# The last layer normalisation of a two-block network: its scaling step divided anew between three engines

## The chip, the cores and the metric

The kernel runs on one core of a Trainium2 chip. The metric is the device time of one execution in microseconds, lower is better. The version before takes 1869.55 us (median of three runs, 1868.58 to 1870.9 us).

## The reference

The program runs two networks one after the other on 512 tokens of width 1024, all in float32: a state-space layer and an attention layer with their feed-forward parts, then two layers of mixed attention. The second network ends each layer with a layer normalisation, and the last of them gives the output. Cut to what matters here:

```
def _layernorm(t, g, b):
    mu = jnp.mean(tf, -1, keepdims=True)
    var = jnp.mean(jnp.square(tf - mu), -1, keepdims=True)
    out = (tf - mu) * lax.rsqrt(var + LN_EPS) * g + b
...
for layer in range(DEPTH):
    ...
    y = jnp.einsum('bse,ed->bsd', jnp.concatenate([ya, yb, yc], axis=-1), w_out[layer])
    h = _layernorm(DEEPNORM_ALPHA * h + y, ln_g[layer], ln_b[layer])
return h
```

## The kernel before

Activations are kept transposed: the 1024 features lie on 128 partitions in eight tiles, `xT[:, k, :]` for k from 0 to 7, each 128 partitions by 512 tokens. So the gain `g` and the shift `b` of a tile are one number for each partition (`column(name, k)`, a column of `vecs`), while mean and root differ along the 512 tokens. The mean over features is a product with a matrix of ones on TensorE, which leaves the same row on all partitions: bank 7 gets the sum that corrects the mean, bank 6 the sum of squares.

Each engine has its own written-out order of instructions, and they meet at semaphores. The normalisation `layer_norm(m, ...)` is called three times, m = 0, 1, 2. Only the last call (`last`) is changed, and it is the end of the program. Its work after the last product of the output projection is this.

- ScalarE copies the correction of the mean from bank 7 to `acc` (L1044), squares it (L1046), and later makes the root in `R` from the variance in `sd`: a logarithm (L701) and an exponential (L702), both in `inverse_root`.
- "Levelling" subtracts the correction of the mean from a tile. VectorE does it from bank 7 for tiles 0, 1, 2, 3 and 7 (`level`, L1813), GpSimd from `acc` for tiles 4, 5 and 6 (L613, `POOL_LEVELS`). VectorE makes the variance between its second and third levelling (L1834).
- VectorE then scales all eight tiles in order: `xT = xT * gain * R` in one instruction each (`scale`, L1821), with the levelling of tile 7 after the scaling of tile 3.
- ScalarE adds the shift to each tile as it has been scaled (L1053).
- SyncE sends each tile to the output as its shift has been added (L509): eight transfers of 256 KB, in order 0 to 7. It then waits for all of them, which ends the program.

In the calls that are not last, the loop over tiles also makes two halves of each tile for the next product; the change leaves these as they are.

Of the kernel before, what the change touches and what calls it, by code (L numbers as in the profile page):

```python
# [18 lines left out]
ACT = mybir.ActivationFunctionType  # L19
ALU = mybir.AluOpType  # L20
# [5 lines left out]
KD = D // P  # L26
# [118 lines left out]
def build(nc, x_in, pos, vec, con, ssm_par, ssm_b, ssm_c, ssm_d, w_in, w_glu, w_gu0, w_dn0, w_a, w_q, w_k, w_v, w_o, w_gu1, w_dn1,  # L145
# [21 lines left out]
    n = 0  # L167
# [13 lines left out]
    xT = everywhere.tensor("xT", [P, KD, S])  # L181
# [4 lines left out]
    tiny = everywhere.tensor("tiny", [P, 64])  # L186
# [4 lines left out]
    R = common.tensor("R", [P, S])  # L191
    VM = Region(nc, common.base + common.at, 8 * KB).tensor("VM", [P, 2, QP, P])
    acc = common.tensor("acc", [P, S])
    sd = common.tensor("sd", [P, S])
# [28 lines left out]
    def column(name, k=0):  # L223
        return vecs[:, VEC[name] + k:VEC[name] + k + 1]
# [92 lines left out]
    sp = Region(nc, common.base, 10 * KB).tensor("sp", [P, 2, 10 * P])  # L317
# [34 lines left out]
    wbfL = common.tensor("wbfL", [P, 2, KD * 4], F32R)  # L352
    CENTRED = (0, 1, 3, 2, 4, 5, 6, 7)
    POOL_LEVELS = (4, 5, 6)
    square_sum = T[:, 0, :]
    squares = (sq[:, 0, :], sq[:, 1, :], T[:, 1, :], T[:, 2, :])
    lat = Oall[:, :, :].rearrange("p a b -> p (a b)")
# [35 lines left out]
    with ExitStack() as ctx:  # L393
        sems = {}

        def sem(name):
            if name not in sems:
                sems[name] = ctx.enter_context(nc.semaphore(name))
            return sems[name]

        banks = [ctx.enter_context(nc.psum_tensor(f"bank{n}", [P, S], F32)) for n in range(8)]
# [9 lines left out]
        def _(sp):  # L411
# [92 lines left out]
                for name in ("qk", "v", "mixed", "out"):  # L504
                    stream(f"{name}{layer}")

            for j in range(KD):
                sp.wait_ge(sem("ln_h"), 8 * 2 + j + 1)
                sp.dma_start(out[j * P:(j + 1) * P, :], xT[:, j, :]).then_inc(sem("out_written"), 16)  # L509
            sp.wait_ge(sem("out_written"), 16 * KD)  # L510

# [1 line left out]
        def _(pool):  # L513
            step = Steps(pool, sem("pool_steps"))
# [94 lines left out]
            def level(m):  # L609
                pool.wait_ge(sem("ln_delta_copied"), m + 1)  # L610
                pool.wait_ge(sem("ln_sq"), 8 * m + 8)
                for k in POOL_LEVELS:
                    nc.gpsimd.tensor_tensor(xT[:, k, :], xT[:, k, :], acc[:, :], ALU.subtract).then_inc(sem("ln_levelled"), 1)  # L613

            for layer in range(2):
# [25 lines left out]
                def add_later(side, to, a, b):  # L641
                    return nc.gpsimd.tensor_tensor(later[:, side, to:to + P], sp[:, side, a:a + P], b, ALU.add)

                pool.wait_ge(sem("shares_ready"), 2 * STEPS * (layer + 1))
                for p in range(2):
# [5 lines left out]
                    for side in range(2):  # L651
# [2 lines left out]
                        add_later(side, P, SOFF[1] + P, sp[:, side, SOFF[2]:SOFF[2] + P])  # L654
                        add_later(side, 2 * P, SOFF[1] + 2 * P, later[:, side, 0:P]).then_inc(sem("stick_later"), 1)
            level(2)

        @block.scalar
        def _(act):
            def ahead(st, i, u, last):  # L660

                v = u + 2
                if v >= st.n:
                    v -= st.n
                    if not last:
                        i = i + 1
                    elif st.name in following:
                        st, i = following[st.name], 0
                    else:
                        return  # L670
                split_high(st, i, v)
# [8 lines left out]
            step = Steps(act, sem("act_steps"))  # L680
# [18 lines left out]
            def inverse_root(o, bank, scale, made, eps=0):  # L699

                step(nc.scalar.activation(o, bank, ACT.Ln, scale=scale, bias=tiny[0:o.shape[0], eps:eps + 1]))  # L701
                nc.scalar.activation(o, o, ACT.Exp, scale=-0.5).then_inc(made, 1)  # L702
# [319 lines left out]
            def layer_norm(m, name, last=False):  # L1022
                st = stages[name]
                blocks = 3 if name.startswith("dn") else 1
                nc.scalar.preload_act_table_set("natural_log_exp_and_others")

                def centred_square(n):
                    at = CENTRED.index(n)
                    act.wait_ge(sem("ln_centred"), 8 * m + at + 1)
                    if at >= 4:  # L1030
                        act.wait_ge(sem("ln_sq_used"), 7 * m + at - 3)
                    nc.scalar.activation(squares[at % 4], xT[:, n, :], ACT.Square).then_inc(sem("ln_sq"), 1)

                for n in range(KD):
                    for b in range(blocks):
                        if n < KD - 1 or b < blocks - 1:
                            ahead(st, n // 4, n % 4 * blocks + b, n >= 4)
                    if n == 2:
                        act.wait_ge(sem("ln_part"), m + 1)
                        nc.scalar.activation(sd[:, :], banks[7][:, :], ACT.Copy, scale=1.0 / (2 * P)).then_inc(sem("ln_mean"), 1)  # L1040
                    for k in {3: (0, 1, 3), 4: (2, 4), 5: (5,), 6: (6,), 7: (7,)}.get(n, ()):
                        centred_square(k)
                act.wait_ge(sem("ln_delta"), m + 1)
                nc.scalar.activation(acc[:, :], banks[7][:, :], ACT.Copy, scale=1.0 / D).then_inc(sem("ln_delta_copied"), 1)  # L1044
                act.wait_ge(sem("ln_delta_copied"), m + 1)
                nc.scalar.activation(sd[:, :], acc[:, :], ACT.Square).then_inc(sem("ln_delta_square"), 1)  # L1046
                act.wait_ge(sem("ln_variance"), m + 1)
                inverse_root(R[:, :], sd[:, :], 1.0, sem("ln_root"), eps=1)
                shift = ("ln_in_b", "ln_b0", "ln_b1")[m]
                for k in range(KD):  # L1050
                    act.wait_ge(sem("ln_scaled"), 8 * m + k + 1)
                    if last:
                        nc.scalar.activation(xT[:, k, :], xT[:, k, :], ACT.Identity, bias=column(shift, k)).then_inc(sem("ln_h"), 1)  # L1053
                        continue
                    nc.scalar.activation(xH[:, k, :], xT[:, k, :], ACT.Identity, bias=column(shift, k)).then_inc(sem("ln_high"), 1)
                    if k == 4:
                        ahead(st, 1, 4 * blocks - 1, True)

            def evict(st, i, u, to, func=ACT.Copy):
                ahead(st, i, u, i == st.turns - 1)  # L1060
                act.wait_ge(w_used, st.block(i, u) + 3)
                return nc.scalar.activation(to, banks[(tiles[st.name] + u) % 4][:, :], func)

            layer_norm(0, "dn1")
            for layer in range(2):
                st = stages[f"qk{layer}"]
# [87 lines left out]
                for s in range(STEPS):  # L1154
                    m, j = divmod(s, QT)
# [65 lines left out]
                stick_weights(1, 2)  # L1221
                gated_high(7)
                layer_norm(layer + 1, f"out{layer}", layer == 1)

        @block.vector
        def _(dve):
            step = Steps(dve, sem("dve_steps"))
# [314 lines left out]
            for i in range(st.turns):  # L1542
                for u in range(st.n):
                    ahead(st, i, u, i == st.turns - 1)
                    if u % 3 == 2:
                        j = 4 * i + u // 3
# [95 lines left out]
            scale = 1.0 / math.sqrt(DN + DR)  # L1642
# [106 lines left out]
            def layer_norm(m, name, bank_of, last=False):  # L1749
                gain, shift = (("ln_in_g", "ln_g0", "ln_g1")[m], ("ln_in_b", "ln_b0", "ln_b1")[m])  # L1750
# [61 lines left out]
                def level(k):  # L1812
                    nc.vector.scalar_tensor_tensor(xT[:, k, :], banks[7][:, :], -1.0 / D, xT[:, k, :], ALU.mult, ALU.add)\  # L1813
                      .then_inc(sem("ln_level"), 1)

                def scale(k):
                    if k in POOL_LEVELS:
                        dve.wait_ge(sem("ln_levelled"), 3 * m + POOL_LEVELS.index(k) + 1)
                    else:
                        dve.wait_ge(sem("ln_level"), 5 * m + min(k, 4) + 1)  # L1820
                    nc.vector.scalar_tensor_tensor(xT[:, k, :], xT[:, k, :], column(gain, k), R[:, :], ALU.mult, ALU.mult)\  # L1821
                      .then_inc(sem("ln_scaled"), 1)

                def low(k):
                    dve.wait_ge(sem("ln_high"), 8 * m + k + 1)
                    nc.vector.scalar_tensor_tensor(xL[:, k, :], xT[:, k, :], column(shift, k), xH[:, k, :].bitcast(F32),
                                                   ALU.add, ALU.subtract).then_inc(h_ready, 1)
# [7 lines left out]
                level(2)  # L1835
                level(3)
                dve.wait_ge(sem("ln_root"), m + 1)
                for k in range(KD):
                    scale(k)
                    if k and not last:  # L1840
                        low(k - 1)
                    if k == 3:
                        level(KD - 1)
                if last:
                    return
                low(KD - 1)
                block_ahead(KD - 1, blocks - 1)
                dve.wait_ge(h_ready, 56 + 16 * m)
# [2 lines left out]
                dve.wait_ge(sem("ln_h"), 8 * m + 8)  # L1851

            layer_norm(0, "dn1", lambda n: banks[(tiles["dn1"] + n) % 4][:, :])
            for layer in range(2):
                lam, sub_gain = tiny[:, 20 + layer:21 + layer], tiny[:, 22 + layer:23 + layer]
# [37 lines left out]
                bias = vecs[0:4, VEC[f"bf{layer}"]:VEC[f"bf{layer}"] + 1]  # L1893
# [63 lines left out]
                for s in range(STEPS):  # L1957
                    m, j = divmod(s, QT)
# [868 lines left out]
```

## Time and profile before

| what | value |
|---|---|
| median of three runs | 1869.55 us (1868.58 to 1870.9) |
| the profiled execution's own time | 1869.21 us |
| its span, first to last instruction | 1867.2 us |
| outside the span | 2.0 us |
| TensorE busy | 1821.6 us, 98% of the span |
| VectorE, ScalarE, GpSimd busy | 1046.7, 838.0, 199.7 us |
| first scaling of the last normalisation starts | 1857.68 us |
| first and last output transfer issued | 1859.45 and 1864.7 us |

The span is the profiled execution's time from its first instruction to its last; the two differ by what lies around it. Busy times are sums of the durations of an engine's instructions, which can overlap by some hundredths of a microsecond when one follows the other without a wait. A number such as L1821 is a line of the kernel before.

### The profile page before, as it was taken

The page shows a single profiled execution, that of the slowest core. Times are in us where ns is not written, and L with a number is a line of the kernel's source. Part 1 is how long each engine was busy: PE and PEld are TensorE (multiplying, and loading weights), DVE is VectorE, ACT ScalarE, POOL GpSimd, SP SyncE. Part 2 cuts the span into 40 slices and gives each one's busy share as a digit, 9 for nine tenths or more (in the row PEclk, how much of TensorE's full clock was granted, in tenths as well). Part 3 has the DMA queues.
Part 4 walks back from the last instruction along what each step waited for, and adds up shares of the span by engine and source line. Part 5 has one row for each costly group of instructions (what it writes and reads, how often), then busy time and mean ns, then how long its engine had stood idle before and what let it go on. Part 6 is the DMA issues. An engine that isn't in the chain of part 4 may idle for free.

```text
span 1867.2 us, 24330 instructions
## 1 busy us (share of the span) xinstructions
PE 1821.6 (98%) x8918; PEld 1407.2 (75%) x8918; DVE 1046.7 (56%) x1633; ACT 838.0 (45%) x1402; POOL 199.7 (11%) x269
## 2 busy tenths in 40 slices
PE   9999999999999999999999999989999989999997
PEld 6787878888887766677888888768666767866675
DVE  8893454444334767755444434465565476556647
ACT  5323344443224667644434422232467633255753
POOL 7880000000000000000000000023000112200000
PEclk9989999999999999999999999999999999999998
DMA  6222223232333111122232333323111122311111
GB/s 211 77 84 79 91 90 101 90 101 91 94 100 103 44 34 28 61 68 93 98 98 93 100 93 94 97 87 99 64 50 53 46 90 88 104 50 54 57 45 57
DMA packets 58764, 152.21 MB, mean 82 GB/s; under 512 B 17152, under 2 KB 22048, under 8 KB 58672
## 3 DMA queue, kind: packets, MB, share of 16 engines
q1 hardware_dynamic: 55120, 148.27, 24.9%
q0 software_dynamic: 3552, 2.70, 0.5%
q8 instruction: 59, 0.97, 0.2%
q14 instruction: 33, 0.27, 0.0%
HBM read 143.79 MB, written 4.19 MB: 79 GB/s over the span
## 4 chain that ended last, share of the span: by engine, by line
PE 91%; DVE 5%; ACT 3%; issue 1%; DMA 0%; POOL 0%; DVEq 0%; SPq 0%; ACTq 0%
PE bank L2018 19%; PE bank L2019 19%; PE bank L2020 19%; PE bank L2511 3%; PE bank L2513 3%; PE bank L2512 3%; PE bank L2488 2%; PE bank L2476 2%; PE bank L2475 2%; PE bank L2474 2%; PE bank L2243 1%; PE bank L2271 1%; PE bank L2598 1%; PE bank L2526 1%; DVE wl L1244 1%
## 5 line engine op out<-in xcount | busy, mean ns | idle before, releaser
L1244 DVE TENSOR_TENSOR wl<-raw,wh 128x1024 fp32r<-128x1024 f32 (+3 forms) x280 | 327.0, 1168 | 492.9 <-ACT wh L677 489.7
L677 ACT ACTIVATE wh<-raw 128x1024 fp32r<-128x1024 f32 (+3 forms) x280 | 279.2, 997 | 571.9 <-PE bank L2020 497.1
L2018 PE MATMUL bank<-xH,wh 128*128 128x512 f32 x904 | 355.9, 394 | 4.0 <-DVE wl L1244 2.1
L2020 PE MATMUL bank<-xH,wl 128*128 128x512 f32 x904 | 352.4, 390 | 0.0
L2019 PE MATMUL bank<-xL,wh 128*128 128x512 f32 x904 | 352.2, 390 | 0.0
L2018 PEld LDWEIGHTS bank<-xH,wh 128*128 128x128 f32 x904 | 170.1, 188 | 43.0 <-issue 3.3
L2019 PEld LDWEIGHTS bank<-xL,wh 128*128 128x128 f32 x904 | 170.1, 188 | 35.4 <-issue 1.0
L2020 PEld LDWEIGHTS bank<-xH,wl 128*128 128x128 f32 x904 | 169.9, 188 | 35.5
L2018 PE MATMUL bank<-hidH,wh 128*128 128x512 f32 x352 | 137.3, 390 | 0.0
L2020 PE MATMUL bank<-hidH,wl 128*128 128x512 f32 x352 | 136.9, 389 | 0.0
L2019 PE MATMUL bank<-hidL,wh 128*128 128x512 f32 x352 | 136.9, 389 | 0.0
L2511 PE MATMUL bank<-xH,wh 128*128 128x512 f32 x256 | 108.4, 423 | 0.0
L2513 PE MATMUL bank<-xH,wl 128*128 128x512 f32 x256 | 100.7, 393 | 0.0
L2512 PE MATMUL bank<-xL,wh 128*128 128x512 f32 x256 | 100.2, 391 | 0.0
L613 POOL TENSOR_TENSOR xT<-xT,acc 128x512 f32<-128x512 f32 x9 | 11.2, 1268 | 737.0 <-ACT acc L1044 737.0
L1916 DVE TENSOR_REDUCE least<-bank 128x1 f32<-128x128 f32 (+3 forms) x96 | 42.6, 486 | 73.3 <-PE bank L2495 73.2
L1100 ACT ACTIVATE Pm<-bank,least 128x128 f32<-128x128 f32 (+3 forms) x96 | 49.7, 523 | 68.4 <-DVE least L1916 68.3
L2019 PEld LDWEIGHTS bank<-hidL,wh 128*128 128x128 f32 x352 | 66.1, 188 | 13.9 <-issue 0.2
L2018 PEld LDWEIGHTS bank<-hidH,wh 128*128 128x128 f32 x352 | 66.1, 188 | 13.9 <-issue 0.2
L2020 PEld LDWEIGHTS bank<-hidH,wl 128*128 128x128 f32 x352 | 66.1, 188 | 13.8
L852 ACT ACTIVATE hidH<-T 128x512 f32 (+1 forms) x44 | 27.8, 632 | 78.3 <-DVEq L1532 78.3
L603 POOL COPY xT<-T 128x512 f32<-128x512 f32 x8 | 8.9, 1107 | 455.1 <-DVE T L1550 455.1
(447 smaller groups left out, 3329.6 us busy)
## 6 DMA issues: line engine op xcount, KB each, us to landing
raw<-w_gu_dram SPq DMA_DIRECT2D x88, 512.0 KB, 3.3
raw<-w_p_dram SPq DMA_DIRECT2D x64, 512.0 KB, 3.4
raw<-w_dn_dram SPq DMA_DIRECT2D x32, 448.0 KB, 3.3
raw<-w_glu_dram SPq DMA_DIRECT2D x16, 512.0 KB, 3.3
raw<-w_dn_dram SPq DMA_DIRECT2D x16, 512.0 KB, 3.5
raw<-w_out_dram SPq DMA_DIRECT2D x16, 512.0 KB, 3.3
raw<-w_in_dram SPq DMA_DIRECT2D x8, 512.0 KB, 7.6
raw<-w_o_dram SPq DMA_DIRECT2D x8, 512.0 KB, 3.4
```

Of the source, the lines that this page charges most:

```text
L677: nc.scalar.activation(wh[:, (st.base + u) % 2, 0:kts * P], raw[:, (st.base + u) % 4, 0:kts * P], ACT.Copy).then_inc(w_high, 1)
L1100: nc.scalar.activation(Pm[side][:, POFF[j]:POFF[j] + w], banks[side][:, 0:w], ACT.Exp, scale=-1.0, bias=least[:, j, side:side + 1], accum_ ...
L1244: nc.vector.tensor_tensor(wl[:, s, 0:kts * P], raw[:, (st.base + u) % 4, 0:kts * P], wh[:, s, 0:kts * P].bitcast(F32), ALU.subtract).then_ ...
L1916: nc.vector.tensor_reduce(least[:, j, side:side + 1], banks[side][:, 0:(j + 1) * P], AX, ALU.min)\
L2018: nc.tensor.matmul(bank, wh[:, s, w], hi[:, k, :], start=first and kt == 0, stop=False)
L2019: nc.tensor.matmul(bank, wh[:, s, w], lo[:, k, :], start=False, stop=False)
L2020: ins = nc.tensor.matmul(bank, wl[:, s, w], hi[:, k, :], start=False, stop=last and kt == kts - 1)
L2474: nc.tensor.matmul(o, xH[:, k, rows], wh[:, s, w], start=k == 0, stop=False)
L2475: nc.tensor.matmul(o, xH[:, k, rows], wl[:, s, w], start=False, stop=False)
L2511: nc.tensor.matmul(bank, wh[:, s, w], xH[:, kt, :], start=kt == 0, stop=False)
L2512: nc.tensor.matmul(bank, wh[:, s, w], xL[:, kt, :], start=False, stop=False)
L2513: ins = nc.tensor.matmul(bank, wl[:, s, w], xH[:, kt, :], start=False, stop=kt == KD - 1)
```

## The change

In the last normalisation alone:

- ScalarE makes the root twice from the same logarithm: an exponential into bank 5 (PSUM), then one into `R` (SBUF). Each raises `ln_root`.
- VectorE multiplies tiles 0, 1, 2, 3 and 7 by the root in bank 5, without the gain. Tile 7 is still levelled after tile 2.
- GpSimd, after its three levellings, multiplies tiles 4, 5 and 6 by the root in `R`.
- Gain and shift are applied together: by ScalarE for tiles 0, 1, 2, 4, 5, 6 (an activation with scale and bias), by VectorE for tiles 3 and 7 (a `tensor_scalar` with multiply and add).
- SyncE sends the tiles in the order 0, 1, 2, 4, 5, 3, 7, 6.

```diff
+    OUT_DVE, OUT_ACT = (3, 7), (0, 1, 2, 4, 5, 6)
 # SyncE
-            for j in range(KD):
-                sp.wait_ge(sem("ln_h"), 8 * 2 + j + 1)
+            for j in (0, 1, 2, 4, 5, 3, 7, 6):
+                if j in OUT_DVE:
+                    sp.wait_ge(sem("ln_scaled"), 22 + OUT_DVE.index(j))
+                else:
+                    sp.wait_ge(sem("ln_h"), 17 + OUT_ACT.index(j))
                 sp.dma_start(out[j * P:(j + 1) * P, :], xT[:, j, :]).then_inc(sem("out_written"), 16)
 # GpSimd
             level(2)
+            pool.wait_ge(sem("ln_levelled"), 9)
+            pool.wait_ge(sem("ln_root"), 4)
+            for k in POOL_LEVELS:
+                nc.gpsimd.tensor_tensor(xT[:, k, :], xT[:, k, :], R[:, :], ALU.mult).then_inc(sem("ln_levelled"), 1)
 # ScalarE
-                inverse_root(R[:, :], sd[:, :], 1.0, sem("ln_root"), eps=1)
+                if last:
+                    step(nc.scalar.activation(R[:, :], sd[:, :], ACT.Ln, bias=tiny[:, 1:2]))
+                    nc.scalar.activation(banks[5][:, :], R[:, :], ACT.Exp, scale=-0.5).then_inc(sem("ln_root"), 1)
+                    nc.scalar.activation(R[:, :], R[:, :], ACT.Exp, scale=-0.5).then_inc(sem("ln_root"), 1)
+                else:
+                    inverse_root(R[:, :], sd[:, :], 1.0, sem("ln_root"), eps=1)
+                if last:
+                    for k in OUT_ACT:
+                        if k in POOL_LEVELS:
+                            act.wait_ge(sem("ln_levelled"), 10 + POOL_LEVELS.index(k))
+                        else:
+                            act.wait_ge(sem("ln_scaled"), 17 + k)
+                        nc.scalar.activation(xT[:, k, :], xT[:, k, :], ACT.Identity, scale=column("ln_g1", k), bias=column(shift, k))\
+                          .then_inc(sem("ln_h"), 1)
+                    return
                 for k in range(KD):
                     act.wait_ge(sem("ln_scaled"), 8 * m + k + 1)
-                    if last:
-                        nc.scalar.activation(xT[:, k, :], xT[:, k, :], ACT.Identity, bias=column(shift, k)).then_inc(sem("ln_h"), 1)
-                        continue
 # VectorE
                 dve.wait_ge(sem("ln_root"), m + 1)
+                if last:
+                    for k in (0, 1, 2, 3, KD - 1):
+                        dve.wait_ge(sem("ln_level"), 5 * m + min(k, 4) + 1)
+                        nc.vector.tensor_tensor(xT[:, k, :], xT[:, k, :], banks[5][:, :], ALU.mult).then_inc(sem("ln_scaled"), 1)
+                        if k == 2:
+                            level(KD - 1)
+                    for n, k in enumerate(OUT_DVE):
+                        dve.wait_ge(sem("ln_scaled"), 20 + n)
+                        nc.vector.tensor_scalar(xT[:, k, :], xT[:, k, :], column(gain, k), column(shift, k), ALU.mult, ALU.add)\
+                          .then_inc(sem("ln_scaled"), 1)
+                    return
                 for k in range(KD):
                     scale(k)
-                    if k and not last:
+                    if k:
                         low(k - 1)
                     if k == 3:
                         level(KD - 1)
-                if last:
-                    return
```

## Rows read from the trace of the kernel before

**Rows 1.** The page: span, and busy time of each engine.

```profile
span 1867.2 us, 24330 instructions
PE 1821.6 (98%) x8918; PEld 1407.2 (75%) x8918; DVE 1046.7 (56%) x1633; ACT 838.0 (45%) x1402; POOL 199.7 (11%) x269
```

**Rows 2.** Chain of waits, 1856 to 1868 us: start, duration, engine and line.

```profile
1857.02 0.64 ACT R L702
...
1857.68 2.97 DVE xT L1821 x4
1860.66 0.60 DVE xT L1813
1861.26 0.67 DVE xT L1821
...
1861.95 2.71 ACT xT L1053 x4
```

**Rows 3.** Timeline of the end: start, duration, engine, instruction, count [idle before].

```profile
1854.39 3.73 POOL L613 TENSOR_TENSOR xT<-xT,acc 128x512 f32<-128x512 f32 x3 [62.51 <-ACT acc L1044]
1856.15 1.28 DVE L1813 SCALAR_TENSOR_TENSOR xT<-bank,xT 128x512 f32<-128x512 f32 x2
1857.68 2.97 DVE L1821 SCALAR_TENSOR_TENSOR xT<-xT,vecs,R 128x512 f32<-128x512 f32 x4 [0.26 <-ACT R L702]
1858.70 2.71 ACT L1053 ACTIVATE xT<-xT,vecs 128x512 f32<-128x512 f32 x4 [1.05 <-DVE xT L1821]
1859.45 5.57 SPq L509 DMA_DIRECT2D out_dram<-xT  x8
```

**Rows 4.** One line at a time, L1821, L1813, L702: duration in ns, smallest, median, largest.

```profile
L1821 DVE SCALAR_TENSOR_TENSOR xT<-xT,vecs,R x8: 736/740/985, 1857.7 to 1863.2; 128x512 f32<-128x512 f32 x8
L1813 DVE SCALAR_TENSOR_TENSOR xT<-bank,xT x15: 678/681/692, 1212.8 to 1860.6; 128x512 f32<-128x512 f32 x15
L702 ACT ACTIVATE R<-R x28: 629/630/632, 28.9 to 1857.0; 128x512 f32<-128x512 f32 x28
```

**Rows 5.** The same view, lines nearest to the new instructions.

```profile
L776 ACT ACTIVATE bank<-pf x1: 602/602/602, 33.9 to 33.9; 128x512 f32<-128x512 f32 x1
L690 ACT ACTIVATE xH<-xT,vecs x24: 722/725/727, 156.3 to 851.8; 128x512 fp32r<-128x512 f32 x24
L1797 DVE TENSOR_TENSOR xT<-xT,bank x18: 686/687/689, 1104.7 to 1851.8; 128x512 f32<-128x512 f32 x18
L1850 DVE TENSOR_SCALAR xT<-xT,vecs x16: 478/478/480, 1229.2 to 1552.7; 128x512 f32<-128x512 f32 x16
L613 POOL TENSOR_TENSOR xT<-xT,acc x9: 1255/1269/1276, 1212.9 to 1856.8; 128x512 f32<-128x512 f32 x9
L523 POOL TENSOR_TENSOR tp<-Cz,pw x4: 2015/2028/3016, 65.8 to 120.3; 128x1024 f32<-128x1024 f32 x4
```

**Rows 6.** The output transfers, L509, and what SyncE waited for.

```profile
L509 SPq DMA_DIRECT2D out_dram<-xT x8: 332/332/344, 1859.5 to 1864.7; - x8
DMA to landing us min/median/max: 2.0/2.1/2.1
SPq L509 <- ACT xT L1053: 40.8, 8, 38.0
```

**Rows 7.** Stretches: us; PE, PEld, DVE, ACT, POOL busy; clock; DMA share; GB/s.

```profile
1860.00:1860.40 0.40, 0.00 (x0) 0.00 (x0) 0.40 (x1) 0.40 (x2) 0.00 (x0) 0.50 0.27 102
1860.40:1861.40 1.00, 0.00 (x0) 0.00 (x0) 1.00 (x3) 1.00 (x2) 0.00 (x0) 0.50 1.00 373
1863.00:1863.40 0.40, 0.00 (x0) 0.00 (x0) 0.40 (x2) 0.40 (x2) 0.00 (x0) 0.50 0.15 51
1863.40:1863.80 0.40, 0.00 (x0) 0.00 (x0) 0.40 (x1) 0.40 (x1) 0.00 (x0) 0.50 0.67 256
1866.00:1866.40 0.40, 0.00 (x0) 0.00 (x0) 0.00 (x0) 0.00 (x0) 0.00 (x0) 0.50 0.75 287
12.00:16.00 4.00, 4.00 (x20) 3.28 (x19) 3.90 (x9) 3.98 (x8) 3.53 (x7) 1.00 1.03 420
```

**Rows 8.** Timeline elsewhere: two runs of instructions back to back.

```profile
1229.17 3.25 DVE L1850 TENSOR_SCALAR xT<-xT,vecs 128x512 f32<-128x512 f32 x8
1831.08 1.13 ACT L1032 ACTIVATE sq<-xT 128x512 f32<-128x512 f32 x2
```

## The prediction

> **What bounds the kernel now.** I read the page first: TensorE is busy for 98% of the span and VectorE for 56% [rows 1]. That says what bounds the program as a whole, and nothing of this change, which touches only what comes after the last product. So I read the chain of waits over the last 12 us. It runs through one thing after another without a gap: the root on ScalarE until 1857.66, four scalings on VectorE, the levelling of tile 7, one more scaling, then four shifts on ScalarE until 1864.66 [rows 2]. The reader is to see that the levelling of tile 7 sits in the middle of the output: ScalarE, which shifts a tile in 0.66 us (three steps in 2.71 - 0.72), follows VectorE at its pace and starves once, between 1861.4 and 1861.95.
>
> Then come the transfers, which the chain does not show. SyncE waits for ScalarE before each of the eight [rows 6]; the first goes out at 1859.45, the last at 1859.45 + 5.57 - 0.33 = 1864.69 [rows 3], lands 2.1 us later at 1866.79 [rows 6], and the span ends 0.41 us after, at 1867.2 [rows 1]. The stretches show what the DMA engines did meanwhile. Their share at the start is 0.27 of 0.4 us, so data began at 1860.29, 0.84 us after the first issue. In full flow the share is 1.00 at 373 GB/s. It drops at 1863.0 + 0.15 × 0.4 = 1863.06, resumes at 1863.8 - 0.67 × 0.4 = 1863.53 and ends at 1866.0 + 0.75 × 0.4 = 1866.30 [rows 7]. So four tiles take 2.77 us, 0.69 us each, twice over, with a hole of 0.47 us between: the hole is the levelling of tile 7. The pace of ScalarE (0.66 us) and that of the transfers (0.69 us) are all but equal. **A faster calculation can therefore bring the end forward only by the hole and by an earlier first tile.**
>
> **The change, part by part.** All in the profiled execution's own clock.
>
> *Root.* The logarithm is unchanged. The exponential at 1857.02 now goes to a bank. The nearest row for a write to a bank is 0.60 us, against 0.63 to SBUF [rows 4, 5], so VectorE may start at 1857.65 in place of 1857.68. The second exponential costs ScalarE one instruction; two such activations without a wait between them take 1.13 us together [rows 8], so it starts at about 1857.55 and ends at 1858.18. ScalarE was idle until 1858.70 [rows 3], so this is hidden. Without that cover it would cost its 0.55 us on every tile.
>
> *First tile.* Before, the first scaling took 0.985 us and the others 0.74 [rows 4]. It had two inputs in SBUF and began while GpSimd was still levelling (until 1854.39 + 3.73 = 1858.12 [rows 3]). The levellings with one input in a bank ran beside GpSimd at 0.68 as they do everywhere [rows 3, 4]. The new multiplication has one input in a bank; the nearest row, an addition of a bank, is 0.69 [rows 5]. Tile 0 is then scaled at 1858.34, and ScalarE's first combined step (scale and bias as columns; 0.72 with either alone [rows 4, 5] and I take the same) runs from 1858.37 to 1859.09. The first transfer is issued at **1859.12, 0.33 earlier**. If a second column costs 0.05 more than one, it is 0.28: a column costs about that over none (0.72 against 0.63 and 0.74 against 0.69 for the nearest pairs).
>
> *VectorE after that.* Steps with a bank follow each other at 0.60 us (1.28 - 0.68 [rows 3]). Tiles 1 and 2 start at 1858.25 and 1858.85, the levelling of tile 7 at 1859.45, tile 3 at 1860.05, tile 7 at 1860.65, done at 1861.34. Then two `tensor_scalar` instructions: 0.478 each at a pace of (3.25 - 0.48) / 7 = 0.40 [rows 5, 8]. Beginning at 1861.25, tile 3 is ready at 1861.73 and tile 7 at 1862.13 if nothing disturbs them, or at 1862.25 and 1862.65 if the first is held until GpSimd is done.
>
> *GpSimd.* Three multiplications after the levellings. It waits for the second exponential and for its own end (1858.12) and starts at 1858.25. The nearest row by size is its levelling, 1.27 at a pace of 1.23 [rows 3, 5]. Multiplications of twice the size take 2.02 to 3.02 [rows 5], so 1.01 to 1.51 for half. I take 1.27, as one of the inputs is also the output in both. Tiles 4, 5 and 6 are ready at 1859.52, 1860.75 and 1861.98.
>
> *ScalarE.* Six steps at 0.66: tile 1 ends at 1859.75, tile 2 at 1860.41, tile 4 at 1861.07 (ready long before), tile 5 at 1861.73, tile 6 at 1862.75, waiting for GpSimd.
>
> *SyncE.* Issues at 1859.12, 1859.78, 1860.44, 1861.10, 1861.76 (tile 5), then tile 3 at 1862.28 at the latest, tile 7 at 1862.68, tile 6 at 1863.01, as an issue takes 0.33 [rows 6]. The last is issued 1.68 us earlier than before. Eight transfers as before, none added, and a wait for tile 3 or 7 holds back only tile 6 behind it, which is later anyway.
>
> *Transfers.* Data begin at 1859.12 + 0.84 = 1859.96. At 0.69 us a tile the sixth tile's turn comes at 1863.43, its data are there from 1862.28 + 0.84 = 1863.12; the eighth's turn is 1864.81, against 1863.85. So the engines never starve, and end at 1859.96 + 8 × 0.693 = 1865.50. Adding 1866.79 - 1866.30 = 0.49 to the landing and 0.41 to the end gives a span of 1866.40. **The sum: 0.33 (start) + 0.47 (hole) = 0.80 us.** Of the 1.68 us that the issue gains, 0.88 goes into the queue: the last tile waits 1 us for its turn, and its landing time grows from 2.1 to about 3.0.
>
> The profiled execution's own time is 1869.21 = 1867.2 + 2.0, 0.34 below the median of the runs shown. Less 0.8 it is 1868.4; the median becomes 1869.55 - 0.8 = **1868.75**. The runs themselves spread over 2.3 us, so a measurement can hardly see this. Within 0.2% (3.7 us) is what cannot be told from no change.
>
> A rule of the Trainium skill bears on the queue. The row says 378 GB/s over four tiles (1.05 MB in 2.77 us) with the engines full [rows 7]. The page "SBUF — State Buffer", section "Summary: rules for kernel authors", says to reckon with about 358 GB/s between HBM and SBUF, and with 436 only between places in SBUF. At 358 a tile is 0.73 us by that page, the data end at 1865.8 and the gain would be an estimated 0.5; at 436 it would be about 1.2. The trace lies between the two.
>
> **The rivals.**
>
> *A. The queue is faster when more waits in it.* At the start of the kernel, with many loads of 512 KB issued together, the same engines moved 420 GB/s [rows 7]. Those are reads with rows of 4 KB, these are writes with rows of 2 KB. At 420 a tile is 0.62 us, and the fifth waits for its issue (1861.76 + 0.84 = 1862.60), so the data end at 1862.60 + 4 × 0.624 = 1865.10: a span of 1866.0, gain 1.2, median 1868.35. If the queue held nothing up at all, the last issue decides: 1863.01 + 2.1 + 0.41 = 1865.52, gain 1.7, median 1867.9. For it: the last issues come closer together than any before. Against: share 1.00 at 373.
>
> *B. The hole only moves.* If GpSimd's second or third multiplication or VectorE's last two steps come late, the sixth transfer is issued after 1862.59 (1863.43 - 0.84) and the engines starve again. At 1.51 us each, GpSimd ends at 1858.25 + 4.5 = 1862.8 and a held tile 3 is ready at about 1863.05: a hole of 0.5 us. Gain 0.33, median 1869.2. Tile 5 would also come later, at 1861.3 from GpSimd.
>
> *C. GpSimd becomes the last, and the end is later than before.* The mechanism is the engines sharing SBUF: the first scaling lost 0.25 us to the levelling beside it [rows 3, 4], and GpSimd could lose in turn to VectorE's run of multiplications. The end is later once tile 6 is issued after 1864.69, that is when GpSimd ends after 1864.69 - 0.03 - 0.72 - 0.05 = 1863.89, or each multiplication takes over 1.88 us. If each waits out one VectorE instruction, 1.27 + 0.69 = 1.96, tile 6 is issued at 1864.93 and the span is 1867.44: +0.24, median 1869.8. Against it: GpSimd's three levellings kept their 1.27 beside VectorE's instructions with a bank [rows 3, 5], and the new multiplications have one too. The section "Who interferes with whom" of the Trainium skill's "SBUF — State Buffer" says the same of VectorE instructions with at most one SBUF input, and speaks against the two `tensor_scalar`, which it counts among those that can take both ports. The 478 ns against 690 agree with two ports. That is the bound with tile 3 held, used above, and it changes nothing in the sum.
>
> *D. Nothing is gained.* The start stays at 1859.45 (the bank write is slower, or the combined step costs over 1 us) and the hole stays: median 1869.55. I see no row for it.
>
> **How the numbers follow.** Leaving out what lies outside these cases (below): forecast as worked out 0.55, A 0.2, B 0.14, C 0.06, D 0.05. Time of the likeliest: 1868.7. All cases lie between -1.7 and +0.24 us of 1869.55; half of the spread of the runs shown is 1.2. So the range is 1869.55 - 1.7 - 1.2 = 1866.7 to 1869.55 + 0.24 + 1.2, rounded to 1870.9. No case comes near 3.7 us either way. What is left for that is something outside these cases, 0.03 on each side: faster 0.03, same 0.94, slower 0.03. The code ahead of the last normalisation is unchanged on every engine, so nothing there has a reason to move.
>
> **What would show it.** VectorE's first scaling at 0.69 in place of 0.985. First output issue at 1859.1, last at about 1863.0 (taken from the start of the root, if the whole shifts). DMA share 1.0 in one block of 5.5 us without a hole. The last transfer landing in about 3.0 us. GpSimd's multiplications at 1.27. The prediction is wrong if the block has a hole, if landing times stay at 2.1, or if the median leaves the range, which only work ahead of 1851 us could bring about.

## The result, and the profile after

The changed kernel takes 1873.63 us in the median of 22 runs (1870.45 to 1879.61), the one before 1869.55 us in the median of 22 (1866.83 to 1875.75). The ratio is 1.0023 with a 95% interval of 1.0015 to 1.003: slower by 0.23%, some 4 us. The forecast was 1868.7 us, in a range that ends at 1870.9. It was wrong in sign, and the measured median lies 2.7 us above the end of the range.

The profiled execution after took 1874.54 us of its own, with a span of 1872.7 us. To compare the ends of two executions I count from the start of ScalarE's copy of the mean's correction into `acc` (L1044 before, L1052 after), and call what follows the tail. Before, the copy starts at 1853.72 us by the timeline, so the tail is 1867.2 - 1853.72 = 13.5 us [rows 1]:

```profile
1853.72 0.60 ACT L1044 ACTIVATE acc<-bank 128x512 f32<-128x512 f32 x1 [0.55 <-PE bank L2429]
```

After, by the timeline of the end (start, duration, engine, instruction, count):

```profile
1855.41 0.60 ACT L1052 ACTIVATE acc<-bank 128x512 f32<-128x512 f32 x1 [0.55 <-PE bank L2457]
...
1856.08 3.73 POOL L617 TENSOR_TENSOR xT<-xT,acc 128x512 f32<-128x512 f32 x3 [62.51 <-ACT acc L1052]
...
1860.00 3.73 POOL L664 TENSOR_TENSOR xT<-xT,R 128x512 f32<-128x512 f32 x3 [0.19 <-ACT R L1059]
1860.07 4.52 ACT L1069 ACTIVATE xT<-xT,vecs 128x512 f32<-128x512 f32 x6 [0.21 <-DVE xT L1860]
1860.91 4.65 SPq L513 DMA_DIRECT2D out_dram<-xT  x8
```

The tail is 1872.7 - 1855.41 = 17.3 us: **3.8 us longer**. The other 1.7 us of this one pair lie ahead of it. These two executions differ in TensorE's granted clock ahead of anything that was changed: between 70 and 90 us it is 1.00 of full speed before and 0.57 after. What causes that was not looked for. Over all the profiled executions below, the copy starts anywhere from 1851.61 to 1860.19 us, which is why I compare tails.

Everything that writes the output is nevertheless faster, as forecast. The first transfer is issued 5.50 us after the copy, against 5.73 [rows 3]. The stretches (us; five engines' busy time; clock; DMA share; GB/s) have no hole any more:

```profile
1861.40:1861.80 0.40, 0.00 (x0) 0.00 (x0) 0.40 (x2) 0.40 (x2) 0.40 (x1) 0.50 0.09 36
...
1862.20:1864.00 1.80, 0.00 (x0) 0.00 (x0) 1.80 (x4) 1.73 (x4) 1.53 (x2) 0.50 0.99 364
1864.00:1866.00 2.00, 0.00 (x0) 0.00 (x0) 0.47 (x2) 0.58 (x1) 0.00 (x0) 0.50 1.02 379
1866.00:1867.20 1.20, 0.00 (x0) 0.00 (x0) 0.00 (x0) 0.00 (x0) 0.00 (x0) 0.50 1.01 379
1867.20:1867.60 0.40, 0.00 (x0) 0.00 (x0) 0.00 (x0) 0.00 (x0) 0.00 (x0) 0.50 0.38 138
1867.60:1868.00 0.40, 0.00 (x0) 0.00 (x0) 0.00 (x0) 0.00 (x0) 0.00 (x0) 0.50 0.00 0
1868.00:1872.70 4.70, 0.00 (x0) 0.00 (x0) 0.00 (x0) 0.00 (x0) 0.00 (x0) 0.50 0.00 0
```

Data flow from 1861.8 - 0.09 × 0.4 = 1861.76 to 1867.2 + 0.38 × 0.4 = 1867.35, 11.94 us after the copy, where before it was 1866.30 - 1853.72 = 12.58 [rows 7]. The output is 0.64 us earlier. The last two rows are what the forecast did not have: after 1867.6 nothing moves and nothing computes, and the program goes on for 5 us.

What SyncE waited for says where, but not for whom (engine and line, what it waited for, us in total, times, longest):

```profile
SPq L513 <- ACT xT L1069: 39.2, 5, 37.8
SPq L394 <- PEq L394: 4.6, 1, 4.6
SPq L394 <- DMA out_dram<-xT: 2.3, 1, 2.3
```

L394 is the line of the `with` statement whose end closes the block, where all engines meet. The wait of 4.6 us there is new; it is put down to TensorE. The rows of that one line show who was really late (duration in ns, start in us):

```profile
L394 POOLq EVENT_SEMAPHORE  x2: 17/17/17, 1872.2 to 1872.6; - x2
L394 PEldq DRAIN  x1: 2230/2230/2230, 1854.9 to 1854.9; - x1
L394 POOLq DRAIN  x1: 12106/12106/12106, 1860.0 to 1860.0; - x1
L394 DVEq DRAIN  x1: 1457/1457/1457, 1863.1 to 1863.1; - x1
L394 ACTq DRAIN  x1: 844/844/844, 1863.8 to 1863.8; - x1
L394 SPq COMPARE_BRANCH  x1: 38/38/38, 1867.8 to 1867.8; - x1
```

Each engine drains before it meets the others. TensorE was done at 1857.1. SyncE was through with the output at 1867.8. GpSimd's drain began with its first multiplication and ended at 1860.0 + 12.1 = 1872.1, **8.4 us after its last multiplication** (1860.00 + 3.73 = 1863.73). The same line in the kernel before, where it is L393:

```profile
L393 POOLq DRAIN  x1: 12179/12179/12179, 1854.4 to 1854.4; - x1
...
L393 SPq COMPARE_BRANCH  x1: 38/38/38, 1866.8 to 1866.8; - x1
```

The drain was there already: until 1866.6, 8.5 us after the last levelling at 1858.12 [rows 3], and it ended 0.2 us before the last tile had landed. It was hidden by 0.2 us. The change put three instructions behind the levelling, moved GpSimd's last instruction from 4.40 to 8.32 us after the copy, and the drain with it. Of these 3.92 us 0.2 had been room, which leaves 3.7 of the 3.8 us by which the tail grew.

### The profile page after: what moved, and what is told of

The parts are those of the page before. It is cut to its first block, busy times and chain, and to the rows that moved or that the text cites. A ratio compares the mean times of both kernels' runs of the same rounds, so it can differ in the third digit from the quotient of the medians.

```text
span 1872.7 us, 24332 instructions
## 1 busy us (share of the span) xinstructions
PE 1825.2 (97%) x8918; PEld 1411.3 (75%) x8918; DVE 1042.1 (56%) x1632; ACT 837.7 (45%) x1401; POOL 203.4 (11%) x272
## 4 chain that ended last, share of the span: by engine, by line
PE 88%; DVE 5%; ACT 3%; issue 1%; POOL 1%; DMA 0%; POOLq 0%; DVEq 0%; SPq 0%; ACTq 0%
PE bank L2046 19%; PE bank L2048 18%; PE bank L2047 18%; PE bank L2539 3%; PE bank L2541 3%; PE bank L2540 3%; PE bank L2516 2%; PE bank L2504 2%; PE bank L2502 2%; PE bank L2503 2%; PE bank L2271 1%; PE bank L2299 1%; PE bank L2626 1%; DVE G L1303 1%; PE bank L2554 1%
## 5 line engine op out<-in xcount | busy, mean ns | idle before, releaser
L2048 PEld LDWEIGHTS bank<-hidH,wl 128*128 128x128 f32 x352 | 66.1, 188 | 13.6
```

Source lines behind the costliest of these rows:

```text
L2048: ins = nc.tensor.matmul(bank, wl[:, s, w], hi[:, k, :], start=False, stop=last and kt == kts - 1)
```

## The experiments

All changes are to the kernel before or the changed kernel as said; ratios are to the kernel before on the same chip.

**Without GpSimd's drain.** The changed kernel, with the end of the block made without it:

```diff
-        block = ctx.enter_context(nc.Block())
+        block = ctx.enter_context(nc.Block(no_gpsimd_drain=True))
```

> The tail is read from the start of ScalarE's copy of the correction into acc to the end of the span: 13.5 us before, 17.3 us after the change. Theory 1 (GpSimd's drain): at the end of the block GpSimd drains, which lasts 8.4 us beyond its last instruction, and everybody waits for it; without that drain the end is set by the last transfer, 12.4 us after the copy by the trace of the changed kernel, so the tail is 12.9 to 13.1 us and the median is 0.4 below the kernel before (some 4.3 us below the changed one). Theory 2 (the barrier waits for another engine, TensorE, which the wait view names for 4.6 us): tail stays 17.3. Theory 3 (the loss lies ahead of the tail, in the first 100 us, where the profiled executions already differ by 1.7 us): the tail is as short as theory 1 says or not, but the median stays about 4 us above the kernel before.

Median 1868.51 us, ratio 0.9993 (0.9984 to 1.0001). The copy starts at 1854.46, the span is 1867.3, so the tail is 12.8 us. The multiplications stand where they stood against the copy, from 1859.05 to 1862.78, and the end no longer follows them:

```profile
L394 SPq COMPARE_BRANCH  x1: 38/38/38, 1866.9 to 1866.9; - x1
...
L394 POOLq EVENT_SEMAPHORE  x2: 17/17/17, 1867.2 to 1867.2; - x2
```

Theory 1 holds. Theories 2 and 3 fall: taking the drain away takes the whole loss away, in the tail (0.1 us below the range forecast for it) and in the median. Once more, to narrow the interval:

> The changed kernel without GpSimd's drain at the end, once more, to narrow the interval: by the profile's tail (12.84 us against 13.48) its median should be 0.6 us below the kernel before, 0.03%; one set of runs gave 0.9993 with an interval of 0.9984 to 1.0001. If the gain is 0.8 or more, the changed kernel's calculation also helps somewhere else; if it is nothing, the hole and the start do not show in the time.

Median 1869.75 us, ratio 1.0000 (0.9989 to 1.0011), tail 1868.2 - 1855.34 = 12.9 us. The tail repeats; that the median is below the kernel before is not shown.

**The drain taken from the kernel before.** The same edit there.

> The kernel before without GpSimd's drain at the end. Theory 1: its drain ended 0.2 us before the last transfer landed, so the transfer decides, tail 13.3 to 13.5 us and the median within 0.3 us of before. Theory 2: same. If instead the drain of GpSimd already set the end before the change, the tail shortens by up to 0.3 us.

Median 1870.34 us, ratio 1.001 (1.0 to 1.0019), tail 1867.4 - 1853.84 = 13.6 us. Nothing is gained, as the output was last there. The forecast of theory 1 was a median within 0.3 us of the kernel before; it is 0.75 us above it (1869.59 beside these runs). The tail (13.6 against 13.5) does not have that difference, and the interval touches 1, so I don't count it as an effect.

**The multiplications back on VectorE.** Everything else of the change stays (cut; the numbers that the engines wait for follow the new order).

```diff
+    LAST_DVE, LAST_POOL = (0, 1, 2, 4, 5, 6, 3, 7), ()
...
-            for k in POOL_LEVELS:
-                nc.gpsimd.tensor_tensor(xT[:, k, :], xT[:, k, :], R[:, :], ALU.mult).then_inc(sem("ln_levelled"), 1)
...
-                    for k in (0, 1, 2, 3, KD - 1):
...
+                    for k in LAST_DVE:
```

> The changed kernel with the multiplications of tiles 4, 5, 6 given from GpSimd back to VectorE (order 0, 1, 2, 4, 5, 6, 3, 7, bank 5 as input); GpSimd only levels, as before. Theory 1: GpSimd's last instruction ends 4.4 us after the copy again, its drain 12.9 us after it, the last transfer lands by 12.5, so the tail is 13.4 us and the median is that of the kernel before within 0.5 us. Theories 2 and 3: tail 17.3 or median 4 us above.

Median 1869.86 us, ratio 0.9997 (0.9988 to 1.0006). The tail is 1867.7 - 1854.03 = 13.7 us, 0.3 more than forecast:

```profile
L395 POOLq DRAIN  x1: 12179/12179/12179, 1854.7 to 1854.7; - x1
L395 SPq COMPARE_BRANCH  x1: 38/38/38, 1867.3 to 1867.3; - x1
```

GpSimd's drain ended 12.9 us after the copy, as forecast. SyncE had the output only at 13.3, where 12.5 was forecast, so here the output sets the end: the transfers had two holes, of 0.3 and 0.6 us. VectorE, which now had eight multiplications and a levelling, was busy without a gap from 1857.97 to 1864.35; that this made the holes is my reading. The loss is gone with the multiplications on GpSimd.

**One multiplication left there** (tile 4 on GpSimd, 5 and 6 on VectorE):

> The changed kernel with only tile 4 multiplied by GpSimd, tiles 5 and 6 by VectorE. Theory 1: GpSimd's last instruction ends 5.9 us after the copy, its drain at 14.3, the tail is 14.8 us (between 13.7 with no multiplication there and 17.3 with three), the median about 1.3 us above the kernel before. Theory 2, that it is not the place of the last instruction but the presence of such work after the root: tail 17.3.

Median 1871.14 us, ratio 1.0003 (0.999 to 1.0016), too wide to say anything. The tail is 1870.0 - 1855.44 = 14.6 us: 13.7, 14.6 and 17.3 for none, one and three multiplications, of which the drain sets the last two and the output the first.

```profile
L395 POOLq DRAIN  x1: 9726/9726/9726, 1860.0 to 1860.0; - x1
```

GpSimd's drain ends at 1860.0 + 9.73 = 1869.7, 8.4 us after its one multiplication at 1861.32; SyncE had the output at 1868.1.

**A late instruction that does nothing.** To the kernel before:

```diff
             level(2)
+            pool.wait_ge(sem("ln_h"), 24)
+            nc.gpsimd.memset(sq[:, 0, 0:1], 0.0)
```

> The kernel before, plus one memset of one column by GpSimd after the last shift (10.9 us after the copy); its result is not used. Nothing on the path of the output changes. Theory 1: the drain runs from there: 10.95 + 0.1 + 8.4 + 0.5, a tail of 20.0 us, 6.5 us more than before. Theory 2 and 3: tail 13.5, median unchanged. If the drain is a fixed price of three queued 128x512 instructions and not of the end, the tail grows by less than 1 us.

Median 1875.07 us, ratio 1.0031 (1.002 to 1.0043). A memset of 0.1 us costs 5.5 us in the medians (1869.59 before) and 6.2 in the tail. The timeline and the line of the block's end show how:

```profile
1862.61 0.10 POOL L658 MEMSET sq<- 128x1 f32 x1 [6.60 <-ACT xT L1055]
```

```profile
L393 POOLq DRAIN  x1: 8514/8514/8514, 1862.6 to 1862.6; - x1
L393 SPq COMPARE_BRANCH  x1: 38/38/38, 1864.7 to 1864.7; - x1
```

The output was complete at 1864.7. The drain lasts 8.4 us beyond the memset, and the tail is 1871.3 - 1851.61 = 19.7 us (forecast 20.0). The price follows the place of the last instruction, not its work.

**Where the 8.4 us come from.** Four drains at places where GpSimd idles, in the kernel before:

```diff
             make_v(3)
+            pool.drain()
...
                 level(layer)
+                if layer:
+                    pool.drain()
...
                                 .then_inc(sem("rows_loaded"), 16)
+                if layer:
+                    pool.drain()
...
             level(2)
+            pool.drain()
```

> The kernel before with four more drains on GpSimd's queue: after its last table work near 131 us (before it has issued any transfer), after the levelling of the second normalisation, after the transfers of the second layer, and after the last levelling. Theory 1a (a drain of GpSimd costs about 8.4 us wherever it stands): each of the four rows lasts 8.4 us beyond the instruction in front of it. Theory 1b (the price belongs to transfers that GpSimd issued): the first is short, the later ones 8 us. Theory 1c (the price belongs to the drain at the end of the block alone): all four are short, below 0.5 us, and the tail stays 13.5 us.

One execution, 1871.5 us. The four drains and the one of the block's end:

```profile
L600 POOLq DRAIN  x1: 2469/2469/2469, 130.6 to 130.6; - x1
L619 POOLq DRAIN  x1: 8096/8096/8096, 1535.9 to 1535.9; - x1
L644 POOLq DRAIN  x1: 5756/5756/5756, 1620.5 to 1620.5; - x1
L662 POOLq DRAIN  x1: 3846/3846/3846, 1856.5 to 1856.5; - x1
...
L393 POOLq DRAIN  x1: 47/47/47, 1860.4 to 1860.4; - x1
```

A drain's row starts while the instructions in front of it still run, so what counts is what lies beyond them. The first stands behind 2.36 us of work and adds nothing: GpSimd had issued no transfer yet. The second ends 4.4 us after the levelling (1535.94 + 3.74) and the third 4.1 us after the last transfer was issued (1622.15). The fourth adds 0.1 us to a levelling of 3.74, though the same levelling is followed by 8.4 in the kernel before. None of 1a, 1b and 1c has it quite: the price belongs to GpSimd's transfers, as 1b says, but it is paid once for each. Between start and second drain it issued 52 (positions, averaging matrices, and 50 in the first layer), between second and third 50, after that none. 4.35 / 52 and 4.1 / 50 are 0.084 and 0.082 us a transfer; 8.4 / 102 is 0.082. The tail, 1869.6 - 1855.90 = 13.7 us, is again set by the output: SyncE was through at 1869.0, GpSimd at 1860.4.

> The kernel before with every transfer that GpSimd issues left out: the tables of cosines and sines, positions, averaging matrices, exchanged rows and the rows for the forget gates are replaced by zeros set by GpSimd or left at one, and the semaphores raised by hand, so the output is not the reference's. Theory 1b (the drain waits for the descriptors or rings of GpSimd's own transfers): the last drain is below 1 us beyond the last instruction. Theory 1a: it is 8.4 us as before. The tail is 13.1 to 13.5 us by both.

One execution, 1867.44 us. All of GpSimd's transfers are left out and zeros stand in place of what they brought, so its output is not the network's:

```profile
L393 POOLq DRAIN  x1: 3829/3829/3829, 1852.9 to 1852.9; - x1
```

The levelling in front lasts 3.73 us: 0.1 us beyond it, as 1b says. The tail is 1865.7 - 1852.21 = 13.5 us.

Half of the transfers drained early, with the late memset to make the rest visible (the drain stands behind the row transfers, for `layer == 0` alone):

> The kernel before with the late memset of the third experiment, and an early drain in the first of the two layers alone, after 52 of GpSimd's 102 transfers. By 0.082 us a transfer the last drain has 50 left, 4.1 us beyond the memset: tail 10.95 + 0.15 + 4.1 + 0.5 = 15.6 us, against 19.7 without the early drain. Rival, that a drain is all or nothing (any transfer since the last one costs 8.4): 19.7. Rival, that any drain before takes the whole price away: 13.5.

```profile
1863.97 0.10 POOL L660 MEMSET sq<- 128x1 f32 x1 [6.59 <-ACT xT L1057]
```

```profile
L393 POOLq DRAIN  x1: 4262/4262/4262, 1864.0 to 1864.0; - x1
```

One execution, 1870.54 us. The memset ended at 1864.07, the drain at 1868.26: 4.2 us for 50 transfers. The tail is 1868.4 - 1852.98 = 15.4 us, forecast 15.6. Then, with the late memset again, all drained early, and 20 small ones added and waited for:

```diff
                                 .then_inc(sem("rows_loaded"), 16)
+                if layer == 1:
+                    pool.drain()
+                    for n in range(20):
+                        pool.dma_start(u_dram[n, 0, 0:1, :], cons[0:1, 0:NCH]).then_inc(sem("extra_written"), 16)
+                    pool.wait_ge(sem("extra_written"), 320)
```

> The third experiment's kernel (memset after the last shift) with an early drain after GpSimd's last transfers, and behind that drain 20 more transfers of 256 bytes each, to a place that nobody reads, waited for at once. By a price of 0.082 us for each transfer since the last drain, finished or not, large or small, the last drain lasts 1.6 us beyond the memset, and the tail is 10.95 + 0.15 + 1.6 + 0.5 = 13.2, hidden behind the transfers of the output: 13.5. By a price for the packets or bytes that they moved, or for transfers still under way, it lasts 0.1 to 0.2 us.

```profile
1866.69 0.10 POOL L663 MEMSET sq<- 128x1 f32 x1 [6.59 <-ACT xT L1060]
```

```profile
L393 POOLq DRAIN  x1: 1812/1812/1812, 1866.7 to 1866.7; - x1
```

One execution, 1870.94 us. 1866.7 + 1.8 is 1.7 us beyond the memset (1866.79), 0.086 for each of 20 transfers of 256 bytes that had landed more than 200 us earlier, or 0.08 with the 0.1 us of a drain without transfers taken off. So it is neither bytes nor transfers under way. The tail is 1869.1 - 1855.68 = 13.4 us, forecast 13.5.

**The drain made early.** The changed kernel, with one drain behind GpSimd's last transfers, and the kernel before with the same:

```diff
                                 .then_inc(sem("rows_loaded"), 16)
+                if layer == 1:
+                    pool.drain()
```

> The changed kernel with one more drain of GpSimd, after its last transfers (near 1622 us, where it then idles until the stick-breaking sums). Theory 1b, sharpened by the earlier rows: a drain costs 0.082 us for each transfer that GpSimd has issued since its last drain (102 in all: 8.4; 52: 4.3; 50: 4.1). The early drain then lasts about 8.4 us beyond the last transfer, hidden, and the one at the end about 0.1 us beyond the last multiplication; the tail is 12.8 to 13.0 us, 0.6 us less than before, and the median between 0.5 and 1.2 us below the kernel before, 4 to 5 below the changed one. Rival: the drain pays for what ran since, not for transfers: tail 17.3 us.

> The kernel before with the same early drain. The transfers set the end in it already by 0.2 us, so the tail stays at 13.4 to 13.5 us and the median within 0.3 us of before. Beside the run above it gives what the new calculation is worth with the drain out of the way: 0.6 us by the tails.

The changed kernel with it: median 1869.95 us, ratio 1.0000 (0.9987 to 1.0012). The loss of 4 us is gone. By its line of the block's end and that of the early drain:

```profile
L645 POOLq DRAIN  x1: 9991/9991/9991, 1624.8 to 1624.8; - x1
L394 POOLq DRAIN  x1: 3765/3765/3765, 1864.8 to 1864.8; - x1
L394 SPq COMPARE_BRANCH  x1: 38/38/38, 1873.1 to 1873.1; - x1
```

8.4 us are paid beyond the issue of the last transfer (1626.40), where GpSimd would have stood idle for over 140 us anyway, and nothing behind the 3.73 us of multiplications. Its tail is 1873.5 - 1860.19 = 13.3 us rather than the 12.8 to 13.0 forecast. In this execution the last tile took 3.2 us to land, against 2.7 after the change, with all issues at the same distance from the copy; why, I did not find out. The kernel before with the early drain: median 1869.67 us, ratio 0.9997 (0.9987 to 1.0007), tail 1868.0 - 1854.57 = 13.4 us. So the new calculation is worth 0.6 to 0.7 us by the two tails without the drain (12.8 and 12.9, against 13.5 and 13.6), and 0.1 by the pair with the early drain; no set of runs shows it in the time. **No version is shown to be faster than the kernel before**; three of the changed one (without the drain, with the early drain, and VectorE alone) can't be told from it.

## Why the prediction was wrong

- **The step that failed** is the last of the sum: "Adding 1866.79 - 1866.30 = 0.49 to the landing and 0.41 to the end gives a span of 1866.40". It took the end of the program to be the last landing plus a constant. The end is the later of two, the landing and the last engine's drain, and GpSimd's had 0.2 us of room. After the change it is 4.3 us later than the landing. I had followed the chain of waits to the last shift and the transfers from there, and never asked when each engine was done with the block's last line; the number was in the trace of before. For the same reason the prediction's last sentence failed, that only work ahead of 1851 us could bring the median out of the range: the tail alone did.
- **The cover was not costed.** GpSimd's work was judged by when its tiles are ready (1859.52, 1860.75, 1861.98 forecast, and it is within 0.1 us of that, counted from the copy). That three more instructions on an idle engine delay its own last one by 3.9 us was not taken for a cost at all.
- **Rival C** named the right engine and the wrong mechanism. Its point of decision, 1.88 us for each multiplication, is far from the 1.27 measured; the end was later all the same. The chance of 0.03 for slower was what was left after cases that all missed the drain.
- **The output path was right in mechanism, somewhat large in size.** The start came 0.23 us earlier, not 0.33: ScalarE's step with scale and bias takes 0.80 us, where I took 0.72. The hole closed. The transfers set the pace, at 0.70 us a tile, in one block of 5.6 us. In all 0.64 us, forecast 0.80. The last issue came 1.28 us earlier, at 1865.10, not 1.68, and the last landing took 2.7 us, forecast 3.0. Rivals A, B and D fall with that, as far as the output goes.
- **The bank** did what was assumed: five multiplications at 0.68 us with none lengthened, beside a GpSimd that kept its 1.27. One of the last two `tensor_scalar` was held: 1.08 us, the other 0.53.
- **Slips in the sums**, none of which moves the forecast. The upper end of the range is 1870.99, not 1870.9. A `tensor_scalar` held until GpSimd's end at 1861.98 and then taking its 0.478 is ready at 1862.46, not 1862.25; the 0.27 us that the prediction allowed had no row, though the held one was in fact ready 0.29 us after GpSimd's end. And 436 GB/s reckoned as in rival A gives a gain of 1.3, not 1.2.

```profile
L1860 DVE TENSOR_TENSOR xT<-xT,bank x5: 676/679/686, 1859.3 to 1862.3; 128x512 f32<-128x512 f32 x5
L664 POOL TENSOR_TENSOR xT<-xT,R x3: 1268/1271/1276, 1860.0 to 1862.5; 128x512 f32<-128x512 f32 x3
L1069 ACT ACTIVATE xT<-xT,vecs x6: 798/800/813, 1860.1 to 1863.8; 128x512 f32<-128x512 f32 x6
L1865 DVE TENSOR_SCALAR xT<-xT,vecs x2: 533/805/1077, 1862.9 to 1863.9; 128x512 f32<-128x512 f32 x2
```

These rows give the durations of the new instructions. The first `tensor_scalar`, started at 1862.94 while GpSimd multiplied until 1863.73, is the one of 1.08. In the run with the multiplications back on VectorE, where GpSimd's last instruction is over by then, neither is held:

```profile
L1865 DVE TENSOR_SCALAR xT<-xT,vecs x2: 540/543/546, 1863.4 to 1863.8; 128x512 f32<-128x512 f32 x2
```

So the hold comes from GpSimd's multiplication. That agrees with the Trainium skill, "SBUF — State Buffer", section "Who interferes with whom", by which a `tensor_scalar` can run in a mode that takes the pair of ports shared with GpSimd, and the one that comes later then blocks. The section has it block until the other is through. The row is 0.54 us longer, where GpSimd had 0.79 left, so these rows don't confirm that part.

## What to carry to other kernels

Ask of the end of a program when each engine is through, drains included, and not only when the output has landed; work moved late onto an idle engine moves that engine's end. In this kernel GpSimd's drain costs 0.08 us for each transfer that GpSimd has issued since its last drain, so either its last instruction comes early enough, or a drain where it idles pays the bill ahead. When a wait at the meeting of all engines is put down to an engine that was long done, look at that line's rows for all engines.

## What the runs showed of the hardware

- A drain of GpSimd lasts about 0.082 to 0.086 us for each transfer that GpSimd itself issued since the one before (0.1 us for none, 1.7 for 20, 4.1 and 4.2 for 50, 4.4 for 52, 8.4 for 102). It is the same for transfers of 256 bytes as for the kernel's own, and the same right behind the last issue (the early drain) as hundreds of microseconds after they had landed. The counts of 20 and 52 rest on one execution each, that of 50 on two. What it does for each transfer, the runs don't show.
- The drains of the other engines at the same place after the change last 0.8 us (ScalarE), 1.5 us (VectorE) and 2.2 us (TensorE), counted from their start beside work still running.
- An activation with a column as scale and another as bias takes 0.80 us on 128x512 from SBUF to SBUF, where one with a single column takes 0.72; the exponential, with none, takes 0.61 to 0.63.
